# Moving the state, y and turning products of the second mixer inside its wide projection tiles

## The reference, cut to what matters

```
z, xbc, dt = split(t @ w_in)                       # t: latent and context tokens
xbc = silu(conv_centred(xbc, conv_w, conv_b))      # 5 taps along the tokens
xs, B, C = split(xbc);  dt = softplus(dt + dt_bias)
# for both directions d, per group and head:
w     = (C @ B^T) * exp(segment sums of dt * A)    # 256 x 256 decay-weighted products
y     = w @ (x * dt) + (C @ state^T) * exp(cs)     # state comes from the context tokens
state = B^T @ (x * dt * tail)                      # over the context tokens
out   = rms_norm(y * silu(z)) @ w_out
```

## Time and profile before

| | us |
|---|---|
| median of 3 runs (2073.78 to 2076.98) | 2076.85 |
| the profiled execution, whole time | 2077.5 |
| its span in the profile | 2075.6 |
| PE busy | 2018.0 (97%) |
| DVE busy | 1457.6 (70%) |
| the loop over groups, second mixer | about 1100 to 1882 |

### The profile page before, as it was taken

One profiled execution on the slowest core, in us unless ns is written; L12 is line 12 of the kernel. 1 busy time (PEld: TensorE's weight loads), 2 busy tenths in 40 slices (PEclk: granted clock), 3 DMA queues, 4 the chain that ended last, 5 costly groups with the idle time before them and its releaser, 6 DMA issues.

```text
span 2075.6 us, 31012 instructions
## 1 busy us (share of the span) xinstructions
PE 2018.0 (97%) x10458; PEld 1676.9 (81%) x10458; DVE 1457.6 (70%) x2076; ACT 968.0 (47%) x1398; POOL 665.3 (32%) x568
## 2 busy tenths in 40 slices
PE   5998999999999999999999999999999999999998
PEld 3567888888888888878878888888888888888886
DVE  5248877777777777773348877787878787787544
ACT  3144444455445444553355445445444544456443
POOL 1035666556656556535100111111112111110011
PEclk7999999999999999999999999999999999999999
DMA  9996676666666666655353554554554645556654
GB/s 354 335 263 140 173 186 174 170 174 167 175 174 179 174 175 174 165 141 165 102 152 99 148 148 125 144 148 124 142 149 114 167 116 147 137 149 199 226 184 154
DMA packets 422706, 349.23 MB, mean 168 GB/s; under 512 B 13600, under 2 KB 366464, under 8 KB 422016
## 3 DMA queue, kind: packets, MB, share of 16 engines
q1 hardware_dynamic: 397552, 273.43, 45.8%
q0 software_dynamic: 19968, 70.26, 14.2%
q10 hardware_dynamic: 5136, 4.89, 0.7%
HBM read 344.21 MB, written 4.33 MB: 168 GB/s over the span
## 4 chain that ended last, share of the span: by engine, by line
PE 86%; DVE 6%; ACT 2%; DMA 2%; issue 2%; POOL 1%; SPq 0%; DVEq 0%; ACTq 0%; POOLq 0%
PE bank L373 22%; PE bank L377 22%; PE bank L375 22%; PE bank L2303 3%; PE bank L2305 2%; PE bank L2304 2%; DVE w_lo L357 2%; DMA arena<-in_na_ada_w_dram 2%; PE bank L2107 1%; PE bank L2241 1%; PE bank L2222 1%; DVE arena L1647 1%; PE bank L1995 1%; PE bank L2236 1%; PE bank L2022 1%
## 5 line engine op out<-in xcount | busy, mean ns | idle before, releaser
L373 PE MATMUL bank<-act_hi,w_hi 128*128 128x512 f32 (+1 forms) x2448 | 905.9, 370 | 10.6 <-DVE w_lo L357 6.2
L377 PE MATMUL bank<-act_hi,w_lo 128*128 128x512 f32 (+1 forms) x2448 | 888.7, 363 | 0.0
L375 PE MATMUL bank<-act_lo,w_hi 128*128 128x512 f32 (+1 forms) x2448 | 888.4, 363 | 0.0
L357 DVE TENSOR_TENSOR w_lo<-arena,w_hi 128x2048 fp32r<-128x2048 f32 x184 | 433.6, 2356 | 212.3 <-ACT w_hi L353 147.9
L373 PEld LDWEIGHTS bank<-act_hi,w_hi 128*128 128x128 f32 x2448 | 462.9, 189 | 95.9 <-issue 14.5
L377 PEld LDWEIGHTS bank<-act_hi,w_lo 128*128 128x128 f32 x2448 | 462.7, 189 | 73.3
L375 PEld LDWEIGHTS bank<-act_lo,w_hi 128*128 128x128 f32 x2448 | 463.3, 189 | 68.9
L620 POOL TENSOR_TENSOR acc<-acc,arena 128x512 f32<-128x512 f32 x224 | 330.4, 1475 | 129.3 <-ACT arena L858 120.1
L353 ACT ACTIVATE w_hi<-arena 128x2048 fp32r<-128x2048 f32 x138 | 263.8, 1912 | 85.3 <-PE bank L2305 78.3
L1415 DVE SCALAR_TENSOR_TENSOR arena<-arena,cond_c 128x512 f32<-128x512 f32 x240 | 248.2, 1034 | 60.7 <-DMA arena<-in_ssd_ada_w_dram 37.7
L858 ACT ACTIVATE arena<-arena,cond_c 128x512 f32<-128x512 f32 x256 | 171.4, 721 | 254.9 <-POOL acc L620 153.7
(11 more groups left out here) (253 smaller groups left out, 2157.1 us busy)
## 6 DMA issues: line engine op xcount, KB each, us to landing
arena<-in_ssd_w_in_dram SPq DMA_DIRECT2D x81, 1024.0 KB, 6.0
arena<-in_na_w_in_dram SPq DMA_DIRECT2D x58, 1024.0 KB, 7.2
arena<-in_ssd_ada_w_dram POOLq DMA_DIRECT2D x96, 512.0 KB, 4.0
arena<-in_na_ada_w_dram SPq DMA_DIRECT2D x64, 512.0 KB, 7.9
arena<-in_ssd_w_out_dram SPq DMA_DIRECT2D x32, 1024.0 KB, 5.1
arena<-in_na_ada_w_dram POOLq DMA_DIRECT2D x32, 512.0 KB, 4.1
arena<-in_na_w_out_dram SPq DMA_DIRECT2D x16, 1024.0 KB, 6.2
arena<-cs_scr SPq DMA_DIRECT2D x64, 256.0 KB, 5.4
```

The source lines that it names most:

```text
L357: nc.vector.tensor_tensor(w_lo[:, n0 % 2, :], raw[slot], w_hi[:, n0 % 2, :].bitcast(F32), ALU.subtract).then_inc(s_lo, 1)
L373: nc.tensor.matmul(out[:, 0:cols], hi[:, w], act_hi3[:, k, 0:cols], start=(k == 0), stop=False)
L375: nc.tensor.matmul(out[:, 0:cols], hi[:, w], act_lo3[:, k, 0:cols], start=False, stop=False)
L377: mm = nc.tensor.matmul(out[:, 0:cols], lo[:, w], act_hi3[:, k, 0:cols], start=False, stop=(k == KT - 1))
```

## The change

Only PE's program is changed, and only the order of it; the other engines keep their orders and their waits.

- `products(p)` no longer stands behind the narrow tile. It is issued inside the wide tile that follows, at k = 3, ahead of `turn_x`. `products` of a group's last pair comes into the x tile of pair 0 of the next group at k = 5; of the last pair but one of all, it is issued behind the last narrow tile, ahead of the output tiles, where it was.
- `states(p)` no longer stands behind the wide tile but inside it, at k = 13.
- `turn_b` is issued inside the x tile of pair 0: at k = 5 behind the products there, in the first group at k = 13.

```
-                def turning(p, idx):
+                def inside(p, idx, group, done=None):
                     def parts(k):
...
                         if k == (9 if first and p == 0 else 3):
+                            if done is not None:
+                                products(done, t4)
                             turn_x(p, t4, idx, t6)
+                        if k == 13:
+                            states(p, t4, group)
                     return parts
+                def inside_first(k):
+                    if k == (13 if first else 5):
+                        if not first:
+                            products(-1, t4)
+                        turn_b()
                 if not first:
-                    project(pe, N_SSD, t10, parts=turning(-1, -1))
-                    states(-1, t4, t1.at(0))
+                    project(pe, N_SSD, t10, parts=inside(-1, -1, t1.at(0), -2))
                 project(pe, N_SSD + 1, t10, cols=LAT, tile=w_c if first else None)
-                if not first:
-                    products(-1, t4)
                 for j in range(PAIRS):
-                    project(pe, N_SSD + 2 + 2 * j, t10, parts=turning(j - 1, 1 + j) if j > 0 else None)
-                    if j == 0:
-                        (turning of B)
-                    else:
-                        states(j - 1, t4, t1.at(1))
+                    project(pe, N_SSD + 2 + 2 * j, t10,
+                            parts=inside(j - 1, 1 + j, t1.at(1), j - 2 if j > 1 else None) if j > 0 else inside_first)
                     project(pe, N_SSD + 3 + 2 * j, t10, cols=LAT)
...
-                    if j > 0:
-                        products(j - 1, t4)
...
             end = Turn(base=32)
+            products(-2, end)
```

More of the change, by code:

```diff
@@ L2247, in ssd_group, with turn_b @@
                 t1, t4, t6, t10 = (Turn(),) * 4 if first else (Turn(g, 1), Turn(g, 4), Turn(g, 6), Turn(g, 10))
-                def turning(p, idx):
+                def turn_b():
+                    pe.wait_ge(s_conv, t6.at(1))
+                    for t in range(2):
+                        mm = nc.tensor.transpose(bank[7][:, t * P:(t + 1) * P], b_t[:, 1, t * P:(t + 1) * P],
+                                                 ident[:, :])
+                    mm.then_inc(s_btr, 1)
+                def inside(p, idx, group, done=None):
                     def parts(k):
@@ L2260, in parts @@
                         if k == (9 if first and p == 0 else 3):
+                            if done is not None:
+                                products(done, t4)
                             turn_x(p, t4, idx, t6)
-                    return parts
+                        if k == 13:
+                            states(p, t4, group)
+                    return parts
+                def inside_first(k):
[3 more added lines that the diff above has]
+                        turn_b()
                 if not first:
-                    project(pe, N_SSD, t10, parts=turning(-1, -1))
-                    states(-1, t4, t1.at(0))
+                    project(pe, N_SSD, t10, parts=inside(-1, -1, t1.at(0), -2))
                 project(pe, N_SSD + 1, t10, cols=LAT, tile=w_c if first else None)
-                if not first:
-                    products(-1, t4)
                 for j in range(PAIRS):
-                    project(pe, N_SSD + 2 + 2 * j, t10, parts=turning(j - 1, 1 + j) if j > 0 else None)
-                    if j == 0:
[L2273 to L2277, removed]
-                    else:
-                        states(j - 1, t4, t1.at(1))
+                    project(pe, N_SSD + 2 + 2 * j, t10,
+                            parts=inside(j - 1, 1 + j, t1.at(1), j - 2 if j > 1 else None) if j > 0 else inside_first)
                     project(pe, N_SSD + 3 + 2 * j, t10, cols=LAT)
```

## The result

The changed kernel takes 2122.95 us (median of 5 runs, 2120.68 to 2123.64), the kernel before 2076.11 (5 runs, 2073.37 to 2076.98). The ratio is 1.0225, 95% interval 1.0215 to 1.0236: 47 us slower. The forecast was 2121, with a range of 2108 to 2146.

A forecast was written before the change was run, and what follows sets the result against it. PE sets the pace, with `w_lo` of a wide tile sometimes last. Work moved into wide tiles adds 86.4 us, gaps shrink by 42.2, net +44 on 2077.5: 2121.5, as median 2121; range 2108 to 2146.

The forecast's parts named there:

- The gap and the chain: Between wide tiles: only the narrow tile, 5.74 us, against 7.34 + 0.15 = 7.49 until `w_lo` is used; PE waits 1.75.
- just in time: DVE reaches `combine` 4.3 to 4.4 us behind the wide tile's stream start; `products` are done about 4.0 behind it.
- The cost inside the tile: Wide tile with its turning grows from 11.41 to 14.20 us by `states` 0.86 and `products` 1.93.
- The open question: Dead time of transposes behind `products`: bounded between the whole 0.35 us and half of it, taken the same as now.
- rival E: Cheaper seams with the wait in place: 5 us saved, chain 0.2 shorter, 2110; counted within the forecast's 0.78.
- POOL's clearance: POOL's two steps end before DVE's passes start, clear by 0.2 us, so the chain stays at 7.34.
- Rival A: POOL's steps again overlap DVE's passes: 14 chains pay 0.94 us, seven behind B 1.34; 2144, chance 0.13.
- Behind B: Before pair 0's x tile in 7 groups: `w_lo` ready at +5.9 us, gap 6.05, shorter by 2.48 each.
- The sum: Over the kernel: 86.4 us moved into wide tiles, gaps 42.2 shorter, net +44 us.
- rival D: PE's clock falls at the new waits: some 30 times 5.2 us, 156 us, about 2277; chance 0.03.
- B: Faster: seams get cheaper by 10.5 us, pair 1's x tile loses its 0.5 wait; 2066, chance 0.03.
- C: No change: PE's work and time stay the same, 2077, needing a 5.7 us chain or earlier `w_lo`; chance 0.03.

The follow-up runs named there:

- states_only: Only the states moved inside the wide tile, at k = 13, against the kernel before: 2082.85 us, ratio 1.0034.
- the cut kernel: The changed kernel with two of the five taps of the x tiles' convolution left out: 2083.39 us, 39.6 less than with all taps.

## Why the prediction was right

*The gap and the chain.* The step on which all rests, that a gap of only the narrow tile can't hold a chain of 7.34 us, was right: the chain is 7.36 and the stream follows at 7.53 (7.49 was worked out). That it is the chain and not the insertion is shown by the kernels that change the chain alone. `combine`, forecast to be just in time at 4.3 to 4.4 us behind the stream's start, starts at +4.2 without a wait. One reading ahead of this was too coarse: of the 4.9 us of the earlier trace rows, 3.0 are two waits in the first group, so in the loop the kernel before waits only six times, 0.3 us each. No term of the sum rests on the 4.9.

*The cost inside the tile.* 14.20 was worked out, 14.16 measured. The open question, whether the turning pays the restart behind `products` like a wide matmul, is answered: from L2241's start to the stream behind the turning there are some 1.5 us (the stream begins about 0.1 after L373's 1369.65), which is 0.86, 0.44 and some 0.2 of dead time. Next to nothing was saved at the seam, so rival E had nothing.

*POOL's clearance.* By the prediction's figures the mix would end some 0.25 us behind the tile's end; it ends at +0.31. The add was put at 1.20 and takes 0.74, so it is clear of the passes by 0.6 us and not by 0.2. Rival A did not happen; states_only shows what it looks like where the tile is 2 us shorter.

*Behind B.* The gap was forecast at 6.05. PE and DVE there:

```profile
1422.97 0.28 PE L373 MATMUL bank<-act_hi,w_hi 128*128 128x256 f32 x1
...
1426.66 2.28 DVE L357 TENSOR_TENSOR w_lo<-arena,w_hi 128x2048 fp32r<-128x2048 f32 x1
...
1429.33 0.39 PE L375 MATMUL bank<-act_lo,w_hi 128*128 128x512 f32 x1
```

`w_lo` at 1428.94 is +5.97, the stream starts at 1429.10, +6.13: 0.08 more, from ACT, which is at +0.29 there and not +0.19.

*The sum.* +44 was forecast, +46.8 measured by the medians and 45.8 by the spans of the profiled runs. The spans can be taken apart by the distances between streams. The first group grew by 5.0 us (3.9 by the prediction's terms), each of groups 1 to 6 by 5.9 (5.8), the last by 5.4 (5.6). So of the missing 1.8 us, 1.2 lie in the first group and 0.9 in the six of the loop, where the gaps are 0.02 to 0.09 us longer than forecast (7.51 to 7.58 for 7.49, 6.13 for 6.05); the last group gives 0.3 back. What the first group adds is a small piece of rival D. The first matmuls of pair 2's x tile, and the clock of the stretch behind them:

```profile
1156.30 0.50 PE L373 MATMUL bank<-act_hi,w_hi 128*128 128x512 f32 x1 [4.27 <-DVE w_lo L357]
...
1157.21 0.63 PE L373 MATMUL bank<-act_hi,w_hi 128*128 128x512 f32 x1
...
1157.00:1160.40 3.40, 3.40 (x12) 2.72 (x10) 2.17 (x2) 1.89 (x2) 0.00 (x0) 0.50 0.80 224
```

The tile takes 15.7 us instead of 14.2. In the sum the first group was taken like the others, but there DVE is late by itself and the wait is 4.27 us.

*The rivals.* B and C needed a chain of 5.74 us; the cut kernel reaches 5.86 and comes to 2083. B's 2066 takes the 0.5 us of pair 1's x tile once; in seven groups they would give 2063. A's price was too high: it takes 0.94 us for 14 chains, but in the kernel before only the chain behind pair 3's tile is that much longer (8.29 us), and that behind pair 2's is 7.82. Neither bears on the forecast. D was given 3%, with 156 us as its price. It is nearer than that: 0.6 us more of wait brought 15 stretches, at a third of the price used, since such a stretch is 3.4 us and not 10. With a chain only 0.2 us longer the clock already fell twice, so that the changed kernel kept its clock in the groups behind the first is a matter of some tenths, which the prediction had not worked out: there it was lucky.

## What to carry to other kernels

Work between two uses of a double-buffered operand is not filler: it is the time in which the other engines make the next one ready, so before moving it inside the tile, compare what is left of the gap with the chain from the release of the buffer to the next operand. The busy share can't tell this: at 97% busy, PE had 0.1 to 1.1 us of room in four of five rounds and none in the fifth, and giving 2.8 us away cost 1.75 of them.

A piece moved alone can look nearly free (6.7 us for the states) while the room it takes is what the next piece needed.

## What the runs showed that was not expected

The granted clock fell to 1.2 GHz behind 15 of 18 waits of PE of 2.1 to 2.2 us, and behind none of 18 waits of 1.5 to 1.6 us. The Trainium skill ("TensorE: Matmul & The Clock Gate", What's actually happening) ties the clock to how busy the engine has been; the trace agrees with that in that longer waits brought more falls, and the wait of 2.82 us that brought none shows that the length of the last wait is not all of it. When it falls stays open here.

GpSimd and VectorE slow each other in both directions: the add of squares takes 1.20 us beside VectorE's passes and 0.74 alone, and a `TENSOR_SCALAR` of 256 columns 0.77 instead of 0.35 beside it. Putting the GpSimd step elsewhere on a VectorE that is busy for 78 of 99 us only changed which instruction paid.
